# Attention heads of a two-block layer: one reciprocal per pair of heads, merging on GpSimd, the output weights split during the last heads, one trial product per unit

## What is computed

```python
def chunk_causal_attention(q, k, v):        # 16 heads, q and k of 96, v of 64 features
    for blk in range(S // Q_BLOCK):
        ...
        s = jnp.einsum('bqhd,bkhd->bhqk', qb, k[:, :k_end]).astype(jnp.float32) * scale
        mask = k_chunk[None, :] <= q_chunk[:, None]      # chunks of 64
        s = jnp.where(mask, s, -jnp.inf)
        p = jax.nn.softmax(s, axis=-1).astype(v.dtype)
        outs.append(jnp.einsum('bhqk,bkhd->bqhd', p, v[:, :k_end]))
    return jnp.concatenate(outs, axis=1).reshape(B, S, H * V_HEAD)

def mla(q_c, kv_c, k_pe, pos, ...):
    q = (rms_norm_2(q_c, q_a_g) @ w_uq).reshape(B, S, MLA_HEADS, QK_HEAD)
    kv = (rms_norm_2(kv_c, kv_a_g) @ w_ukv).reshape(B, S, MLA_HEADS, QK_NOPE + V_HEAD)
    ...                                                  # norms per head, rotary part
    return chunk_causal_attention(q, k, v)
```

## Time and profile before

| | us |
|---|---|
| median of 3 runs | 2871.57 (2869.43 to 2874.33) |
| the profiled execution | 2867.9, span of the core 2866.1 |
| TensorE busy | 2669.7 (93%) |
| VectorE busy | 1679.3 (59%) |
| ScalarE busy | 1163.7 (41%) |
| GpSimd busy | 309.4 (11%) |
| up-projection | about 1774 to 1964 |
| sixteen heads | 1965.8 to 2313 |
| splits and output product | 2324 to about 2400 |

### The profile page before, as it was taken

One profiled execution on the slowest core, in us unless ns is written; L12 is line 12 of the kernel. 1 busy time (PEld: TensorE's weight loads), 2 busy tenths in 40 slices (PEclk: granted clock), 3 DMA queues, 4 the chain that ended last, 5 costly groups with the idle time before them and its releaser, 6 DMA issues. The chain is left out here.

```text
span 2866.1 us, 32083 instructions
## 1 busy us (share of the span) xinstructions
PE 2669.7 (93%) x12144; PEld 2103.5 (73%) x12144; DVE 1679.3 (59%) x2168; ACT 1163.7 (41%) x1679; POOL 309.4 (11%) x258
## 2 busy tenths in 40 slices
PE   7999999999999999999999988888999979599993
PEld 5888888888877887777777788877666658477772
DVE  5788888888532323443343323777787853566663
ACT  4234444444431214544524414554333341366661
POOL 0010111100100000000000000222101100342113
PEclk9999999999999999999999999999999989699997
DMA  5333323232335221022122041234321031999987
GB/s 186 110 122 108 106 78 120 92 123 85 108 127 190 71 77 49 30 81 59 30 73 63 24 142 42 85 113 156 100 60 49 20 84 57 362 357 342 358 348 274
DMA packets 209161, 362.66 MB, mean 127 GB/s; under 512 B 51911, under 2 KB 159816, under 8 KB 195320
## 3 DMA queue, kind: packets, MB, share of 16 engines
q1 hardware_dynamic: 193432, 322.94, 32.6%
q0 software_dynamic: 14720, 34.64, 3.2%
q10 hardware_dynamic: 864, 3.15, 0.3%
HBM read 310.72 MB, written 116.93 MB: 149 GB/s over the span
## 5 line engine op out<-in xcount | busy, mean ns | idle before, releaser
L398 PE MATMUL PS<-UHI,WHI 128*128 128x512 f32 x1008 | 415.7, 412 | 4.1 <-DVE ULO L127 4.1
L398 PE MATMUL PS<-ULO,WHI 128*128 128x512 f32 x1008 | 400.2, 397 | 0.0
L398 PE MATMUL PS<-UHI,WLO 128*128 128x512 f32 x1008 | 400.1, 397 | 0.0
L127 DVE TENSOR_TENSOR WLO<-arena,WHI 128x1024 fp32r<-128x1024 f32 x94 | 115.3, 1227 | 214.7 <-ACT WHI L123 214.5
L398 PEld LDWEIGHTS PS<-UHI,WHI 128*128 128x128 f32 x1008 | 190.6, 189 | 52.3 <-issue 5.5
L398 PEld LDWEIGHTS PS<-ULO,WHI 128*128 128x128 f32 x1008 | 190.6, 189 | 47.5 <-issue 5.5
L398 PEld LDWEIGHTS PS<-UHI,WLO 128*128 128x128 f32 x1008 | 190.2, 189 | 46.3
L1496 PE MATMUL PS<-U2HI,WHI 128*128 128x512 f32 x480 | 193.1, 402 | 2.6 <-DVE WLO L127 2.6
L1496 PE MATMUL PS<-U2HI,WLO 128*128 128x512 f32 x480 | 189.6, 395 | 0.0
L1496 PE MATMUL PS<-U2LO,WHI 128*128 128x512 f32 x480 | 189.5, 395 | 0.0
L834 DVE SCALAR_TENSOR_TENSOR RC<-arena,cols,RC 128x1024 f32<-128x1024 f32 x120 | 157.2, 1310 | 10.3 <-issue 0.9
(11 more groups left out here) (466 smaller groups left out, 6054.2 us busy)
## 6 DMA issues: line engine op xcount, KB each, us to landing
arena<-in_w_in SPq DMA_DIRECT2D x88, 512.0 KB, 3.9
xd_dram<-in_x SPq DMA_DIRECT2D x32, 768.0 KB, 6.2
y_dram<-in_x SPq DMA_DIRECT2D x32, 768.0 KB, 6.0
arena<-in_w_gate SPq DMA_DIRECT2D x13, 1024.0 KB
arena<-in_w_up SPq DMA_DIRECT2D x13, 1024.0 KB
arena<-in_w_down SPq DMA_DIRECT2D x13, 1024.0 KB, 12.9
qk_dram<-RA SPq DMA_DIRECT2D x32, 384.0 KB, 2.3
arena<-qk_dram SPq DMA_DIRECT2D x32, 384.0 KB, 4.5
```

The costliest lines, as they stand in the source:

```text
L127: return eng.tensor_tensor(dst, src, hi.bitcast(F32), ALU.subtract)
L398: last = pe.matmul(o[:, h * HALF:(h + 1) * HALF], x[:, k, :], y[:, k, h * HALF:(h + 1) * HALF], start=(k == r == 0), stop=(k == ND - 1 and ...
```

## The change

It has five parts, all in the second block's attention and in what follows it.

- `UPS` does two slices in each of tiles 2 to 5, on both engines.
- TensorE asks for one trial product per unit in units 0 to 7, for `turn_tops` in unit 8, and for `turn_head` in units 9 and 10. ScalarE's `tops_hi` and `features_hi` move behind exponentials 8, 10 and 11.
- `normalize` goes. ScalarE copies (`results`) the sums and the unnormalised values out of PSUM, each 64 partitions by 512, the first half after exponential 6 of the head and the second after exponential 1 of the next. VectorE makes one reciprocal of 128 by 512 per half of a pair of heads, behind the maxima and `tops_lo`. GpSimd multiplies by it, by the gate, and adds, in halves: three operations of 128 by 512 per half.
- `SUMREC` becomes two buffers; the second takes the place of the third diagonal buffer, so `PDIAG` has two. ScalarE waits for `s_merged` before it overwrites `SUMREC` and `YB`.
- `w_out_2` is split during the last two heads: slices 0 to 3 after exponentials 8 to 11 of head 14, slices 4 to 7 after exponentials 1, 3, 5 and 7 of head 15, the low parts on VectorE behind the reciprocals. After `retire` only `RA` is split.

```diff
-        PDIAG = [SQUARES[:, 0:HALF], SQUARES[:, HALF:], part(24 * T + 512, (HALF,))]
+        PDIAG = [SQUARES[:, 0:HALF], SQUARES[:, HALF:]]
-        SUMREC = part(20 * T, (HALF,))
+        SUMREC = [part(20 * T, (HALF,)), part(24 * T + 512, (HALF,))]
-        UPS = {2: (0,), 3: (1, 2), 4: (3,), 5: (4, 5), 6: (6,), 7: (7,)}
+        UPS = {2: (0, 1), 3: (2, 3), 4: (4, 5), 5: (6, 7)}
@@ SyncE
-                        sp.wait_ge(s_merged, t + 1)
+                        sp.wait_ge(s_merged, 2 * t + 2)
@@ TensorE, unit k of head h
-                            if k < 4:
-                                trial(h + 1, 2 * k)
-                                trial(h + 1, 2 * k + 1)
-                            if k == 6:
+                            if k < NT:
+                                trial(h + 1, k)
+                            if k == NT:
                                 turn_tops(h + 1)
-                        if h + 2 < NHEADS and 7 <= k < 9:
-                            turn_head(h + 2, k - 7)
+                        if h + 2 < NHEADS and 9 <= k < 11:
+                            turn_head(h + 2, k - 9)
@@ ScalarE
+                def results(h, half):
+                    t, at, sums = h // 2, h % 2 * 64, 64 - h % 2 * 64
+                    act.wait_ge(s_pv, NUNIT * h + (NUNIT if half else 4))
+                    if t >= 1:
+                        act.wait_ge(s_merged, 2 * (t - 1) + half + 1)
+                    act.activation(SUMREC[half][at:at + 64, :], PS[sums:sums + 64, half, :], ACT.Copy)
+                    act.activation(YB[t % 2][at:at + 64, half * HALF:(half + 1) * HALF], PS[at:at + 64, half, :],
+                                   ACT.Copy).then_inc(s_y, 1)
+                def merge_weights_hi(k):
+                    if k == 0:
+                        act.wait_ge(s_w8, 16)
+                        act.wait_ge(s_vx, NPAIRS)
+                    split_hi(act, W8HI[:, k, :], RB[:, k, :]).then_inc(s_w8hi, 1)
                         exponential(h, k)
-                        if k == 7 and h + 1 < NHEADS:
+                        if k == 1 and h:
+                            results(h - 1, 1)
+                        if k == 6:
+                            results(h, 0)
+                        if h == NHEADS - 2 and k >= 8:
+                            merge_weights_hi(k - 8)
+                        if h == NHEADS - 1 and k < 8 and k % 2:
+                            merge_weights_hi(4 + k // 2)
+                        if k == NT and h + 1 < NHEADS:
                             tops_hi(h + 1)
-                        if 8 <= k < 10 and h + 2 < NHEADS:
-                            features_hi(h + 2, k - 8)
+                        if k >= 10 and h + 2 < NHEADS:
+                            features_hi(h + 2, k - 10)
+                results(NHEADS - 1, 1)
@@ GpSimd, merge(t)
+                    for half in range(2):
+                        at = slice(half * HALF, (half + 1) * HALF)
+                        y = YB[t % 2][:, at]
+                        pool.wait_ge(s_y, 4 * t + 3 + half)
+                        pool.wait_ge(s_sumrec, 2 * t + half + 1)
+                        pool.tensor_tensor(y, y, SUMREC[half], ALU.mult)
+                        pool.drain()
+                        pool.tensor_tensor(y, y, SIG1[t % 2][:, at], ALU.mult)
+                        pool.drain()
+                        pool.tensor_tensor(RA[:, t, at], RA[:, t, at], y, ALU.add).then_inc(s_merged, 1)
+                        pool.drain()
@@ VectorE
+                def reciprocals(t, half):
+                    dve.wait_ge(s_y, 4 * t + 3 + half)
+                    dve.reciprocal(SUMREC[half], SUMREC[half]).then_inc(s_sumrec, 1)
+                def merge_weights_lo(k):
+                    dve.wait_ge(s_w8hi, k + 1)
+                    split_lo(dve, W8LO[:, k, :], RB[:, k, :], W8HI[:, k, :]).then_inc(s_w8lo, 1)
                 for h in range(NHEADS):
-                    if h:
-                        normalize(h - 1, 1)
                     if h + 1 < NHEADS:
                         for i in range(NT):
                             largest(h + 1, i)
-                    normalize(h, 0)
-                    if h + 1 < NHEADS:
                         tops_lo(h + 1)
+                    if h % 2:
+                        reciprocals(h // 2, 0)
+                    elif h:
+                        reciprocals(h // 2 - 1, 1)
                     if h + 2 < NHEADS:
                         features_lo(h + 2, 0)
                         features_lo(h + 2, 1)
-                dve.drain()
-                normalize(NHEADS - 1, 1)
+                    else:
+                        for k in range(4):
+                            merge_weights_lo(4 * (h + 2 - NHEADS) + k)
+                reciprocals(NPAIRS - 1, 1)
@@ next block: the splits of w_out_2 go from ScalarE and VectorE, TensorE's wait too
-                    pe.wait_ge(s_w8lo, k + 1)
-                    split_hi(act, W8HI[:, k, :], RB[:, k, :]).then_inc(s_w8hi, 1)
-                act.wait_ge(s_w8, 16)
-                    dve.wait_ge(s_w8hi, k + 1)
-                    split_lo(dve, W8LO[:, k, :], RB[:, k, :], W8HI[:, k, :]).then_inc(s_w8lo, 1)
```

More of the change, by code:

```diff
@@ L1303, in build @@
         s_y = sem("s_y")
+        s_sumrec = sem("s_sumrec")
+        s_w8hi = sem("s_w8hi")
+        s_w8lo = sem("s_w8lo")
         s_zero7 = sem("s_zero7")
@@ L2413, in _ @@
                         features_lo(h + 2, 1)
[L2414 to L2417 removed]
+                    else:
+                        for k in range(4):
+                            merge_weights_lo(4 * (h + 2 - NHEADS) + k)
+                reciprocals(NPAIRS - 1, 1)
+        retire(s_held)
         BIG = 1e30
```

23 lines of the change are left out of this document (2 added, 21 removed).

## The result

The kernel with the change takes 2834.35 us (median of 4 runs, 2833.31 to 2835.94), the kernel before 2871.42 us in the same session (4 runs, 2869.43 to 2874.33): a ratio of 0.9871 with a 95% interval of [0.9853, 0.9888]. The forecast was 2831.0 us in 2814 to 2852. The profiled execution after has a span of 2833.2 us and took 2835.09.

What follows compares the result with a forecast made beforehand. TensorE was taken as the bound, waiting at group borders, in each head and before the output product. Terms 23.7+0.5+24.4+0.7-2.95-3.3-4.1+0.5+1.15 = 40.6 us, off 2871.6, gave 2831.0 us (2814 to 2852).

Steps and rivals of the forecast that it cites:

- Borders, 23.7: Up-projections: splitting slices 6 and 7 in tile 5 removes TensorE's weight waits at three group borders, 7.9 us each.
- Heads 1 to 13, 24.4: Heads of 19.7 us instead of 22.1, plus a 1.15 us merge wait in six odd heads: 24.4 us gained.
- all 2.65 us: Each head: TensorE's waits for trial products' maxima vanish with one trial per unit and maxima at the front of VectorE's head.
- rival B: Heads: short gaps keep making TensorE's clock fall, 1.1 us in each of 14 heads, giving 2846 us; chance 0.15.
- Head 15: 2.95 and 3.3: Last head: ends 2.95 us later from waits on ScalarE; VectorE's splits and GpSimd's merges taking turns add 3.3 us.
- Head 14, 0.7: Head 14: loses its waits, but exponentials 10 and 11 stand behind w_out_2 splits; 0.7 us gained.
- Tail: 4.1, less 0.5: After the last head: last reciprocal 4.1 us later behind VectorE's splits; the tail itself 0.5 us shorter.
- Start of the output product, 1.15: Output product: one pair of splits less before the first product, so it starts 1.15 us sooner.
- C: Two last heads cost nearly nothing and GpSimd's merge is just in time: 10.5 us of losses gone, 2820 us; chance 0.17.
- D: Group borders still wait, since something other than the place of slices 6 and 7 makes them late: 2855 us; chance 0.06.
- E: Heads don't get shorter, ScalarE taking what VectorE gives back; only the borders gain: 2855 us; chance 0.07.
- F: ScalarE's chain bounds each head at exponentials 2 and 7, costing 69 us: slower, 2900 us; chance 0.05.

Runs made afterwards that it cites:

- e1: The kernel before with only the changed UPS line, two weight slices in each of tiles 2 to 5: 2849.86 us, ratio 0.9917.
- e5: The kernel after with ScalarE's tops_hi moved behind exponential 9: 2837.78 us, ratio 0.9877.
- e6: The kernel after with two trial products per unit in units 0 to 3 again, turn_tops in unit 6: 2830.59 us, ratio 0.9858.
- e11: The kernel after with VectorE's reciprocal of an even head in front of the trial products' maxima: 2836.96 us, a single run.
- e3: The kernel after with only VectorE's half of the w_out_2 splits back behind the last head: 2826.85 us, ratio 0.9844.
- e2: The kernel after with both halves of the w_out_2 splits back behind the last head: 2825.9 us, ratio 0.9843.
- e7: The kernel after with second-half copies after exponential 3 and w_out_2 splits placed where nothing else wants the engines: 2816.12 us, ratio 0.9802.
- e8: e7 with tops_hi behind exponential 9 and the waits for the next block's constants moved later: 2808.38 us, ratio 0.9780.
- e9: The kernel after with only the waits for the next block's constants moved, behind VectorE's first sums and to TensorE's first logits: 2835.53 us, ratio 0.9885.
- e4: The kernel after with ScalarE's copies of a head's second half after exponential 3 instead of 1: 2822.07 us, ratio 0.9823.

## Why the prediction was right, and where its sum was off

The forecast of the profiled execution was 2827.3 us and it took 2835.1; the medians differ by 3.4 us. The sum of 40.6 us belongs to the stretch from A to B, but for some of the 1.15 at the product's start. That stretch gave 34.9; the table in the section on the result has both by stretches. By the steps:

1. *Borders, 23.7.* Measured 22.6 (22.8 in e1 up to the first turn_tops). Right in mechanism and place: no WKVLO wait is left. Missing was the price of being early: head 0's load, which nobody had waited for, is 1.39 us late.

2. *Heads 1 to 13, 24.4.* Measured 23.5. The total is nearly right, its terms are not. The odd heads' wait for the merge costs 1.56, not 1.15: it is a wait of 1.91, of which some 0.35 would be there anyway. In six heads that is 2.5 us more. The even heads take 19.58 where 19.7 was laid out, which gives 1.6 back over thirteen heads. And the layout of a head counted nothing for exponential 9 behind tops_hi; the trace shows 0.74 there, but e5 says that it is worth only 0.18.

3. *Which edit did it.* The prediction put all 2.65 us down to both edits together. e6 and e11 part them: with the old spacing and the maxima in front (e6) nearly all of it is there, and the spacing of the trials brought 0.3 us a head while it made the reciprocal, the merge and thus exponential 2 of odd heads late. The prediction had the merge wait as a cost of the merging on GpSimd; it is as much a cost of the spacing, which was counted as a pure gain.

4. *Clock in the heads (rival B).* The clock is 1.00 in heads 1 to 14, though they keep waits of 0.5 to 1.9 us. B didn't happen. The Trainium skill, "TensorE: Matmul & The Clock Gate" ("A second HAM failure mode: psum-queue depth-cycling"), tells of another kernel whose frequent micro-idles between groups of products made the clock swing; carried over to these heads it would have had the clock fall. The trace of after disagrees. In e11, with a wait of 2.56 us in each even head, two of the periods are 23.5 instead of 22.0, and the clock of two heads is 0.93: it does come down there, in some heads only.

5. *Head 15: 2.95 and 3.3.* Together 6.05 us of wait were expected, 8.22 came, and 1.9 us of low clock behind it that the sum didn't hold; head 15 lost 10.0 us where 6.25 were counted. "The two take turns" was the step that failed: VectorE's four splits ran in 4.55 us, undisturbed, and GpSimd's one operation waited for all four. e3 puts 4.18 us on this. Where both did take turns, in the tail, three of GpSimd's operations took 2.05 each instead of 1.26 and VectorE's four 7.76. The Trainium skill, "SBUF — State Buffer" ("Who interferes with whom"), calls what the two engines share an exclusive lock, and says, of VectorE's two-port modes, that whoever issues first has it for the whole instruction. The trace agrees that one waits for the other, but here the wait lasted for four instructions. The wait without VectorE's splits is 4.04 (e3), and 3.40 without any (e2); it was put at 2.75 with one split of ScalarE's in it.

6. *Head 14, 0.7.* Measured 0.9, so the sum lacks nothing here, but the splits cost more than the 0.2 that was kept for exponentials 10 and 11 behind them: head 14 is 0.6 us shorter in e2, with one wait of 0.45 where after has 0.63 and 0.86.

7. *Tail: 4.1, less 0.5.* The last reciprocal starts 4.0 us after the copies, as counted. The gain of 0.5 from the shorter tail isn't there: without the early splits (e2) the gap from the last values to the first product is 14.86, before it was 14.72. GpSimd's last operation ends 8.8 us after the last values instead of 9.1, but the first split follows 2.3 us behind it instead of 1.8. With the splits it is 17.54: 2.8 more than before, where 4.1 - 0.5 - 1.15 = 2.45 were counted.

8. *Start of the output product, 1.15.* The pair of splits less is worth 1.3 at the first product (e7 against e2). With the constants out of the way B to C is 36.6 to 36.7 (e8, e9) instead of 37.5, but that isn't shown to be the splits' doing. All traces start the product at half the clock: the weight loads take 0.33 us instead of 0.19 for 6.1 us behind B in before, 4.0 in after and e9, 4.3 in e8, and 3.2 in e1, which splits as the kernel before does. Two us less at half the clock are worth 1 us, all of the difference. In after the wait for the constants, 2.02 against 0.60 of idle time before, takes more than this back, so that B to C is 0.6 us longer, not shorter. The prediction moved a step without asking what else the engine behind it waits for.

Against the sum, the borders lack 1.1 us, heads 1 to 13 0.9, head 15 3.8 and the tail 0.35, while heads 0 and 14 gave 0.4 more: together 5.7, the shortfall from A to B (each is read from single traces, to some tenths). The medians miss the forecast by only 3.4 us, and that they come nearer than the stretch is chance: they went down by 37.1 us, the profiled executions by 32.8.

Rivals C, D, E and F are out: the two last heads cost more than counted, the borders' waits went, and the heads got shorter. Some of E's mechanism is there: ScalarE, which the copies load with 2.4 us more a head, holds TensorE up by 0.54 and 0.74 us in each even head, where before it was 0.53, and by more only where it waits for GpSimd.

## What to carry to other kernels

When a slow instruction stands in front of short ones that another engine is waiting for, changing that order can bring what spreading the short ones out does not; spreading them out also makes everything behind them late, so look at what that is. A copy that hands a buffer on should stand as late in its queue as its reader allows: one number moved (after exponential 3 instead of 1) was worth as much as a third of the whole change. Work put into "idle" time of one engine has to be checked against what runs on its neighbours at that moment, and against the few microseconds it can bring at all: here 10 us were paid where 1.3 were to be had.

## What the hardware showed that I had not expected

- VectorE can keep GpSimd out for several instructions. Four subtractions of two 128x1024 SBUF operands ran in 4.55 us, and a GpSimd multiplication of 128x512 that began 0.2 us after the first of them took 5.46 us instead of 1.26. It took 5.45 to 5.48 at the same place in e4, e5, e6 and e9. 22 us later, with the same instructions, the two shared, in these five traces and in e11: 7.76 us for the four, 2.03 for GpSimd's first. GpSimd's began 0.21 to 0.22 us after VectorE's first where it was kept out, and 0.25 to 0.26 after it where they shared. Whether this decides, or something else, isn't settled by these runs.
- VectorE's reciprocal of 128 partitions by 512 takes 3.33 us (from SBUF) against 3.36 for 64 partitions (from PSUM): twice the rows cost nothing here.
- The issue of one DMA of small pieces (128 KB of router weights) held SyncE's queue for 14.1 to 17.4 us in thirteen traces of the same code, and this spread of 3 us reached the time of the kernel wherever someone waited for the loads behind it. The small pieces alone are not the reason: in after the load just ahead, 16 KB laid out the same way, was issued in 0.46 us, and one of 2 KB just behind took 3.50. Nine loads of 512 KB had been issued in the 5 us before, and may be what held the queue; no run parts the two.
- The same length of idle time was followed by different clocks. At the third tile of the output product 2.52 (e2), 2.93 (e1), 3.36 (e5) and 4.18 us (e7) were followed by a clock of 0.89 over the next 15 us, and 2.02 (after), 2.28 (e4) and 2.48 (e6) by 1.00. In head 15 of e2 3.40 was followed by 1.00, while 3.2 in head 0 was followed by 0.50 for the next 3 us in every trace.
